# Who copies the hi part of a weight unit: ScalarE in place of GpSimd

## The reference

```
xn = rmsnorm(x) * g1;  z = xn @ w_in      # rg_x, rg_y, q, k, v, g_lr, g_out, m_a, m_b
xc = causal_conv4(rg_x)
r, i = sigmoid(blockdiag(xc)), sigmoid(blockdiag(xc))
a = exp(-8 * r * softplus(-lam));  b = sqrt(1 - a*a) * i * xc
h_t = a_t * h_(t-1) + b_t;         ya = (h * gelu(rg_y)) @ w_a
o = gated linear attention over q, k, v in chunks, 4 heads, decays from g_lr
yb = (rmsnorm(o) * gn * silu(g_out)) @ w_b
x = x + (sigmoid(m_a) * ya + sigmoid(m_b) * yb) @ w_out
u = rmsnorm(x) @ w_up;  gate, val = split(causal_conv3(u))
x = x + (gelu(gate) * val) @ w_down;      y = rmsnorm(x) * gf
```

## Time and profile before

| | |
|---|---|
| median of 3 runs | 1968.67 us (1965.29 to 1969.84) |
| the profiled execution | 1968.59 us, span 1966.8 us |
| PE busy | 1914.4 us, 97% |
| DVE busy | 906.0 us, 46% |
| POOL busy | 701.9 us, 36% |
| ACT busy | 420.9 us, 21% |
| chain that ended last | PE 92%, DVE 4%, issue 3%, ACT 1% |
| granted TensorE clock, mean | 0.988 |

### The profile page before, as it was taken

The page is one execution under the profiler, slowest core; times in us unless marked ns, Lnnn a source line. Parts: engine busy times, 40 slices in busy tenths (PEclk is TensorE's granted clock), DMA queues, the critical chain, the costliest instruction groups (busy, mean ns, idle before and its releaser), DMA issues.

```text
span 1966.8 us, 29051 instructions
## 1 busy us (share of the span) xinstructions
PE 1914.4 (97%) x11890; PEld 1885.9 (96%) x11890; DVE 906.0 (46%) x916; ACT 420.9 (21%) x480; POOL 701.9 (36%) x324
## 2 busy tenths in 40 slices
PE   7999999999999999999999999999999999999997
PEld 6999888888889999999999999999999999999997
DVE  5211277787865311141134555536253535354546
ACT  4000144555532100020011121102010101010115
POOL 3333232232234343344344333333333333334353
PEclk9999998999999999999999999999999999999999
DMA  5221123222212111131113211111111111111112
GB/s 192 87 89 43 44 88 109 89 77 91 77 43 75 43 43 53 43 130 48 48 48 125 65 44 43 44 54 44 44 44 53 43 44 45 53 43 44 53 52 86
DMA packets 48167, 127.11 MB, mean 65 GB/s; under 512 B 6952, under 2 KB 20008, under 8 KB 48080
## 3 DMA queue, kind: packets, MB, share of 16 engines
q1 hardware_dynamic: 27744, 88.39, 13.5%
q10 hardware_dynamic: 20352, 37.64, 5.5%
HBM read 108.14 MB, written 18.14 MB: 64 GB/s over the span
## 4 chain that ended last, share of the span: by engine, by line
PE 92%; DVE 4%; issue 3%; ACT 1%; DMA 0%; DVEq 0%; SPq 0%
PE acc L416 84%; PE acc L594 1%; PE acc L755 1%; PE small L514 1%; PE small L517 1%; DVE rg_xc_h L1327 1%; PE small L526 1%; DVE rg_xc_h L1324 1%; DVE rg_ext L1149 0%; PE small L607 0%; DVE gla_bc_keT L1214 0%; PE small L755 0%; PE small L489 0%; DMA x_in<-in_x 0%; PE small L533 0%
## 5 line engine op out<-in xcount | busy, mean ns | idle before, releaser
L382 POOL TENSOR_TENSOR w_hi<-w_raw,ones 128x1024 fp32r<-128x1024 f32 x149 | 288.3, 1935 | 1215.5 <-PE acc L416 1203.7
L416 PE MATMUL acc<-xn_hi,w_hi 128*128 128x346 f32 (+1 forms) x2520 | 553.8, 328 | 15.9 <-DVE xn_lo L1136 12.1
L416 PE MATMUL acc<-xn_lo,w_hi 128*128 128x346 f32 (+1 forms) x2520 | 541.8, 323 | 0.0
L416 PE MATMUL acc<-xn_hi,w_lo 128*128 128x346 f32 (+1 forms) x2520 | 540.1, 323 | 0.0
L416 PEld LDWEIGHTS acc<-xn_hi,w_hi 128*128 128x128 f32 x2520 | 427.5, 190 | 21.5 <-issue 12.9
L416 PEld LDWEIGHTS acc<-xn_lo,w_hi 128*128 128x128 f32 x2520 | 429.7, 190 | 0.0
L416 PEld LDWEIGHTS acc<-xn_hi,w_lo 128*128 128x128 f32 x2520 | 428.6, 190 | 0.0
L384 POOL TENSOR_TENSOR w_lo<-w_raw,w_hi 128x1024 fp32r<-128x1024 f32 x149 | 384.2, 2578 | 11.7
L1520 DVE TENSOR_TENSOR residual<-acc,residual 128x1032 f32<-128x1032 f32 x56 | 69.0, 1232 | 115.8 <-PE acc L416 115.8
L1491 DVE SCALAR_TENSOR_TENSOR tmp<-val_ext,ffn_params,tmp 128x1024 f32<-128x1024 f32 x48 | 97.9, 2040 | 39.4 <-ACT tmp L1069 36.6
L1491 DVE SCALAR_TENSOR_TENSOR gate_conv<-gate_ext,ffn_params,gate_conv 128x1024 f32<-128x1024 f32 x48 | 92.0, 1917 | 40.6 <-ACT gate_conv L1063 37.7
(11 more groups left out here) (216 smaller groups left out, 2082.6 us busy)
## 6 DMA issues: line engine op xcount, KB each, us to landing
w_raw<-in_w SPq DMA_DIRECT2D x153, 512.0 KB, 3.5
ha_scratch<-rg_gelu_ha ACTq DMA_DIRECT2D x8, 519.0 KB, 3.5
h<-ha_scratch ACTq DMA_DIRECT2D x8, 519.0 KB, 7.0
residual<-in_x ACTq DMA_DIRECT2D x8, 519.0 KB, 7.6
gla_qk_pair<-qk_scratch ACTq DMA_DIRECT2D x8, 512.0 KB, 5.8
smp_v_rows<-smp_v_scratch ACTq DMA_DIRECT2D x8, 512.0 KB, 6.5
out_gla_sample<-smp_state ACTq DMA_DIRECT2D x8, 512.0 KB, 3.8
smp_state<-in_gla_state ACTq DMA_DIRECT2D x7, 512.0 KB, 5.0
```

The lines of the kernel that those rows point to most:

```text
L382: nc.gpsimd.tensor_tensor(whi[s], raw[s], one, ALU.mult).then_inc(w_hi_done[s], 1)
L416: mm = nc.tensor.matmul(acc[g][:, n, 0:cw], w[s][:, t * P:(t + 1) * P], x[:, c0 + n * cw:c0 + (n + 1) * cw], start=a, stop=z)
```

## The change

The hi copies by GpSimd are kept for units 1 and 2 and for the last three. For the others ScalarE does them with an activation (Copy), in the new function w_high(u): it waits for the load of raw and for TensorE to be done with the slot's last unit, copies, and raises w_hi_done. GpSimd waits for w_hi_done and subtracts, as before. Each w_high is written at one place in ScalarE's order, so its copy is done after what stands ahead of it there: in the recurrent stage one behind line 957 and one behind line 966, in the output gates behind the Silu, in the FFN behind the bias of gate and of value. Excerpt:

```diff
@@ gpsimd
-            with pool.Fori(1, (N_UNITS - GRP) // 2) as i:
-                split(i, 0)
-                split(i, 1)
+            split(1, 0)
+
+            def low(i, s):
+                pool.wait_ge(w_hi_done[s], i + 1)
+                nc.gpsimd.tensor_tensor(wlo[s], raw[s], whi[s].bitcast(F32), ALU.subtract).then_inc(w_split[s], 1)
+            low(1, 1)
+            with pool.Fori(2, (N_UNITS - GRP) // 2) as i:
+                low(i, 0)
+                low(i, 1)
@@ scalar
+            def w_high(u, per=0, i=0):
+
+                s, n = slot_of(u), nth(u, per, i)
+                act.wait_ge(w_loaded[s], 16 * n + 16)
+                act.wait_ge(unit_done[s], n)
+                nc.scalar.activation(whi[s], raw[s], ACT.Copy).then_inc(w_hi_done[s], 1)
...
@@ scalar, recurrent stage
                 nc.scalar.activation(xc, ext[:, 3:3 + C], ACT.Identity, scale=par("w3", j), bias=par("b", j))\
                     .then_inc(xbias_ready, 1)
+                w_high(U_RG + 2, 2, j)
                 act.wait_ge(sS_ready, j + 1)
...
                 nc.scalar.activation(gy[:, late], gy[:, late], ACT.Gelu_apprx_tanh).then_inc(gelu_ready, 1)
+                w_high(U_RG + 3, 2, j)
                 plain()
@@ scalar, output gates
                     nc.scalar.activation(T[s][:, late], T[s][:, late], ACT.Silu).then_inc(silu_done, 1)
+                    w_high(U_GO + 2 + s, 2, i)
                     plain()
...
@@ scalar, ffn_block
                                      bias=fpr[:, bass.ds(3 * UB + F, 1)]).then_inc(gbias_ready, 1)
+                w_high(u + 2, per, i)
                 act.wait_ge(gconv_step, 3 * F + 3)
...
                                      bias=fpr[:, bass.ds(3 * UB + FB + F, 1)]).then_inc(vbias_ready, 1)
+                w_high(u + 3, per, i)
                 act.wait_ge(act_done, F + 1)
```

More of the change, by code:

```diff
@@ L813, in _ @@
                 for s, g in ((0, 1), (1, 0)):
+                    w_high(U_QKV + s + 2, 2, i)
                     act.wait_ge(acc_free[g], G_QKV[g] + i + 1)
@@ L889, in sample_tokens @@
                 nc.scalar.activation(t, bank[0:NS, :], ACT.Copy).then_inc(sT_ready, 1)
+            w_high(U_QKV + 10)
             ke_tokens(0, NMETA)
@@ L894, in _ @@
             load_qk(PAIR, NMETA)
+            w_high(U_QKV + 11)
+            with act.Fori(1, 4) as i:
+                w_high(U_QKV + 10, 2, i)
+                w_high(U_QKV + 11, 2, i)
             act.wait_ge(acc_free[0], G_RG[0])
@@ L1016, in _, with gate_b @@
                 gate_o(i)
-            with act.Fori(0, KB) as j:
+            def gate_b(j):
                 act.wait_ge(acc_free[1], G_B[1] + j + 1)
                 nc.scalar.activation(T[2][:, late], T[2][:, late], ACT.Tanh, scale=0.5).then_inc(tanh_done, 1)
+                w_high(U_B + 2, 2, j)
+            with act.Fori(0, KB - 1) as j:
+                gate_b(j)
+                w_high(U_B + 3, 2, j)
+            gate_b(KB - 1)
             for k in range(KB):
@@ L1027, in _ @@
                 act.dma_start(blkl(HA, k), ha_scr[k][:, late]).then_inc(hl_loaded[k], 16)
+            w_high(U_B + 3, 2, KB - 1)
             for k in range(KB):
@@ L1030, in _, with gate_a @@
                 nc.scalar.activation(blkl(HAH, k), blkl(HA, k), ACT.Copy).then_inc(hah_done, 1)
-            with act.Fori(0, KB) as j:
+            def gate_a(j):
                 act.wait_ge(acc_free[1], G_A[1] + j + 1)
                 nc.scalar.activation(T[2][:, late], T[2][:, late], ACT.Tanh, scale=0.5).then_inc(tanh_done, 1)
+                w_high(U_A + 2, 2, j)
+            with act.Fori(0, KB - 1) as j:
+                gate_a(j)
+                w_high(U_A + 3, 2, j)
+            gate_a(KB - 1)
             act.wait_ge(acc_free[1], G_OUT[1])
@@ L1038, in _ @@
                 if k == KB - 1:
-                    ready(U_OUT - 1)
+                    w_high(U_A + 3, 2, KB - 1)
                     for m in range(KB):
@@ L1045, in _ @@
             for k in range(KB):
+                w_high(U_OUT + k + 2)
                 act.wait_ge(acc_free[1 - k % 2], G_OUT[1 - k % 2] + k // 2 + 1)
@@ L1055, in _, with ffn_block @@
             norm_factor(sum2_mm, lnr2_done, r2_done, LATE)
-            def ffn_block(F, grp):
+            def ffn_block(F, grp, u, per, i):
                 plain()
@@ L1076, in _, with ffn_group, down_high @@
             GU, GD = GRP, KB // 2
-            def ffn_group(F0_, grp, half):
+            NU, ND = 2 * GRP, GRP
+            per = 2 * (NU + ND)
+            def ffn_group(F0_, grp, half, u0, i=0):
                 for f in range(GRP):
-                    ffn_block(F0_ + f, grp + f)
+                    ffn_block(F0_ + f, grp + f, u0 + 2 * f, per, i)
                     ffn_hi(half, f)
+            def down_high(u0, i, n):
+                for v in range(n):
+                    w_high(u0 + NU + v + 2, per, i)
             act.wait_ge(set_f, 4)
-            ffn_group(0, 0, 0)
+            ffn_group(0, 0, 0, U_FFN)
             gper = 2 * (GU + GD)
             with act.Fori(0, NGRP // 2 - 1) as i:
-                ffn_group(2 * GRP * i + GRP, GU + gper * i, 1)
+                ffn_group(2 * GRP * i + GRP, GU + gper * i, 1, U_FFN + NU, i)
+                down_high(U_FFN + NU, i, ND)
                 act.wait_ge(acc_free[0], G_FFN[0] + 2 * GU + GD + gper * i)
-                ffn_group(2 * GRP * i + 2 * GRP, 2 * GU + GD + gper * i, 0)
+                ffn_group(2 * GRP * i + 2 * GRP, 2 * GU + GD + gper * i, 0, U_FFN + 2 * NU + ND, i)
+                down_high(U_FFN + 2 * NU + ND, i, ND)
                 act.wait_ge(acc_free[0], G_FFN[0] + 3 * GU + 2 * GD + gper * i)
             n = NGRP // 2 - 1
-            ffn_group(GRP * (NGRP - 1), GU + gper * n, 1)
+            ffn_group(GRP * (NGRP - 1), GU + gper * n, 1, U_FFN + NU + n * per)
+            down_high(U_FFN + NU + n * per, 0, 1)
             act.preload_act_table_set(LN_EXP)
```

## The result

| | before | after |
|---|---|---|
| median of the runs beside one another | 1968.46 us (1965.29 to 1969.84) | 1940.16 us (1939.9 to 1943.3) |
| the profiled execution | 1968.59 us, span 1966.8 us | 1939.9 us, span 1938.1 us |
| PE busy | 1914.4 us, 97% | 1902.9 us, 98% |
| POOL busy | 701.9 us | 411.5 us |
| ACT busy | 420.9 us | 563.7 us |

The ratio after to before is 0.9862, interval 0.9845 to 0.9879. The forecast was 1946.0 us, so the gain is 6 us larger than it said.

What follows compares the result with a forecast made beforehand. TensorE, busy 97% of the span, was taken as the bound, with seven 3.0 us waits for the recurrent stage's masked scores. Recurrent gain, output-gate wait and FFN loss summed as 1968.6 - 29.2 + 1.35 + 5.3 = 1946.0 us; range 1934 to 1960.

Steps and rivals of the forecast that it cites:

- Removed, 3.65 us an iteration: Recurrent stage: VectorE's two ten-column steps around the scan shrink to 0.22 us each, taking 3.65 us off the chain.
- ScalarE's second copy, 0.7 us on the scores' chain: Recurrent stage: each iteration's second copy on ScalarE delays its following work by 0.7 us, all of it reaching the scores.
- Moved: the subtraction among the convolution steps, a wait of 1.0 us: Recurrent stage: the subtraction runs ahead of the second convolution step; TensorE waits about 1.0 us for the copied outputs.
- The stage: Recurrent stage: seven iterations of 39.2 us take 274.4 us instead of 303.65, a gain of 29.2 us.
- The clock: Recurrent stage: TensorE keeps full clock, granted 1.00, through the new waits of 1.0 us.
- Start of the output gates, 1.35 us once: Start of the output-gate stage: unit 35's copy stands behind the first Silu, so TensorE waits 1.35 us once.
- FFN, 7 x 0.75 = 5.3 us: FFN down groups: the subtraction gets between two VectorE steps, making the residual line 0.75 us later seven times, 5.3 us.
- Everything else at nothing: Other stages: added latency of at most 7.3 us stays under the 11.44 us a unit lasts, so no cost.
- subtraction behind the steps: Rival, chance 0.13: VectorE keeps second and third convolution steps together; new waits and most of unit 35's vanish; 1932 us.
- Half clock stays: Rival, chance 0.11: the recurrent stage's new waits still bring the clock down, 2.3 us each of seven times; 1962 us.
- the gain is eaten: Rival, chance 0.05: the recurrent stage's wait for copied outputs replaces the whole one removed; time within 0.2% of before.
- slower: Rival, chance 0.07: the recurrent stage's small steps don't wait for GpSimd, so nothing comes off the chain; 1983 us.

Runs made afterwards that it cites:

- e5: Changed kernel with ScalarE's first copy of each recurrent iteration moved ahead of the wait for the block's result; 1949.73 us, ratio 0.9901.
- e6: Kernel before with GpSimd's slot 1 splits held behind the convolution in the recurrent stage, and a like hold in each FFN group; 1934.89 us, ratio 0.9824.
- e4: Changed kernel with GpSimd's subtraction held until the convolution steps are done, in the recurrent stage (slot 1) and the FFN; 1935.17 us, ratio 0.983.
- e1: Kernel before with hi copies moved to ScalarE only for the units split in the recurrent stage; 1936.38 us, ratio 0.9836.
- e3: Kernel before, all splits on GpSimd, which in the recurrent stage begins slot 1's split only after the iteration's convolution steps; 1932.41 us, ratio 0.9822.
- e8: Kernel before with GpSimd setting the hi buffer to a constant instead of copying, for slot 1 in the recurrent stage; 1942.54 us, ratio 0.9869.
- e7: Changed kernel with the second unit of each recurrent iteration split by GpSimd alone again; 1939.92 us, ratio 0.9855.

## Why the prediction was right, and where its sizes were off

The mechanism, the stage, the place of each new wait and the clock came as forecast; the measured gain was 6 us larger, since the new waits are about half of what was summed. Two of its signs came out small by that: the wait for the outputs at 0.44 us instead of about 1, and those for the residual at 0.6 and less instead of 0.7 to 0.8. By its steps:

- *Removed, 3.65 us an iteration.* Right: (1.79 - 0.16) + (2.30 - 0.14) = 3.79. ScalarE's copy takes 1.05 us as reckoned, by the mean of 147.
- *ScalarE's second copy, 0.7 us on the scores' chain.* Right in kind, too dear. Line 990 starts 1.92 us after the start of line 986, where the same two stood 1.38 apart before: 0.54 us late, not 0.7. The scores are ready 0.45 us ahead of TensorE and were 3.01 behind it, so they gained 3.46 of the 3.79; only 0.33 us of the delay reached them. The forecast let all of it through because it saw hardly a pause on ScalarE. One is there: in the kernel before line 977 starts at 442.51, 1.31 us after line 973, behind the second gate product on TensorE, which ends there at 442.37; in the kernel after line 998 starts 1.17 us after line 994. That wait takes up 0.14 us of the delay.
- *Moved: the subtraction among the convolution steps, a wait of 1.0 us.* The place is right to the step: it asks during the first and holds up the second. The size is 0.44 us. The steps begin 1.28 us after the first score product instead of 1.7, because the scores are early by what the last point says; and they take 415.10 - 409.03 = 6.07 us instead of 6.4, since the subtraction holds VectorE from 410.33 to 412.56, 2.23 us, where the sum had the whole 2.40 and a full 1.30 for the step behind it. Against that stand 0.15 us between the end of the output copy and the state updates, which the sum left out.
- *The stage.* 269.34 us instead of 274.4. The gain is 303.65 - 269.34 = 34.3 us, not 29.2: this is 5.1 of the 6 us.
- *The clock.* Right. The granted 1.00 holds from 240 to 556 us. It had been argued from a single idle of 1.85 us; the seven waits of 1.5 in e5 now show it for waits of that length. For longer ones e6 shows that no such argument from a single idle holds: 2.54 us kept the clock and 2.24 us didn't.
- *Start of the output gates, 1.35 us once.* Right: 1.25 before the first matmul with the new unit. It begins with the Silu on ScalarE at 558.63, 1.07 us long. VectorE, ScalarE, GpSimd and TensorE there, a timeline each:

```profile
559.74 1.30 DVE L1450 SCALAR_TENSOR_TENSOR tmp<-v_o,params,tmp 128x1038 f32<-128x1038 f32 x1 [2.50 <-ACT tmp L1029]
```

```profile
559.61 1.04 ACT L784 ACTIVATE w_hi<-w_raw 128x1024 fp32r<-128x1024 f32 x1
```

```profile
560.73 2.55 POOL L393 TENSOR_TENSOR w_lo<-w_raw,w_hi 128x1024 fp32r<-128x1024 f32 x1 [21.13 <-ACT w_hi L784]
```

```profile
563.41 0.74 PE L422 MATMUL acc<-xn_hi,w_hi 128*128 128x346 f32 x3 [1.25 <-POOL w_lo L393]
```

- *FFN, 7 x 0.75 = 5.3 us.* Seven waits in the right place, but smaller: 3.9 us in the view of the weight loads against 0.5 before, so 3.4 us (the matmuls' own view has 1.7 us in six; in the recurrent stage it is the weight loads' view that agrees with the time lost). VectorE and GpSimd in one down group, beside the earlier trace rows and the last of the earlier trace rows:

```profile
1232.83 4.63 DVE L1535 SCALAR_TENSOR_TENSOR tmp<-val_ext,ffn_params,tmp 128x1024 f32<-128x1024 f32 x2 [1.57 <-ACT tmp L1103]
```

```profile
1233.71 2.66 POOL L393 TENSOR_TENSOR w_lo<-w_raw,w_hi 128x1024 fp32r<-128x1024 f32 x1 [8.63 <-ACT w_hi L784]
```

The pair of steps takes 4.63 us where it took 4.19, 0.44 more, and the sum had 4.94: the same 0.3 too much for a held step as in the recurrent stage.

- *Everything else at nothing.* Right: of the waits for a split only the one of 1.3 us was added.
- *Not in the forecast:* the clock's stretch at the entry of the stage, 6.8 us in this profile and 3.4 in that of before, costs 1.7 us here. Together, 34.3 - 1.3 - 3.4 - 1.7 = 27.9 us of the 28.7 by which the spans differ. Of the other 0.8 us, 0.6 is in the waits for xn_lo at the start of the kernel, 11.5 us here and 12.1 before; over the eleven profiles they vary from 11.2 to 12.1.

Of the rivals, "subtraction behind the steps" was the nearest after the forecast: e4 makes it real and has 1935.17 us, where the rival's sum said 1932. Its profiled execution has 1936.81: the stretch of 13.7 us at the entry instead of 3.4 is worth up to 5 us there, and the wait of 1.3 at unit 35, which the rival let go for the most part, stayed. "Half clock stays" fell with the granted 1.00 of the kernel after, and e5 keeps the clock with waits of 1.5; "the gain is eaten" fell with waits of 0.44 us for the outputs in place of 3; "slower" fell with e1 and e3.

## What to carry to other kernels

When a tiny VectorE operation lasts some us, look at what GpSimd reads at that moment: an operation with two inputs in SBUF and a reading GpSimd instruction take turns, and whichever asks while the other runs goes next. The cure is to move GpSimd's instruction in time, to where VectorE copies out of PSUM or is idle; one wait in GpSimd's own order (e3) gave 35 us, while giving the work to another engine gave 28. That brought three new waits, of 3.0 us in the recurrent stage, 1.3 at unit 35 and 3.4 in the FFN, and the last two come with the 131 copies that hadn't been in anybody's way. Cost such a move stage by stage, since here 16 of 147 copies held all of the gain and the rest a loss of 4 to 6 us.

## What the runs showed of the hardware that had not been expected

- A wait of 3.0 us on TensorE among small matmuls brought the clock down to its lower level (1.2 GHz) each of seven times, for 3.4 us (four times) or 6.8 us (three times), and cost some 2.0 us on average on top of itself. Waits of 1.4 to 1.6 us, fourteen times in e5 and e8, left it at 2.4 GHz. In between the length alone doesn't decide: in e6 an idle of 2.24 us was followed by 3.4 us at the lower level, and one of 2.54 us by none.
- What the waits of the recurrent stage cost is in the view of the weight loads, not in that of the matmuls: over the seven iterations of the recurrent stage e5, e8, after and e7 take 12.3, 11.3, 3.0 and 2.1 us more than e3, where the weight loads' entries are 12.6, 11.5, 3.1 and 2.1 and the matmuls' 10.5, 9.5, 1.4 and none.
- The clock at the entry of the recurrent stage, behind a stretch in which TensorE was busy for 2.40 of 4 us in the kernel after, is at its lower level for 3.4, 6.8 or 13.7 us, and for one and the same kernel for 6.8 or 13.7.
- A held VectorE step costs less than the GpSimd instruction that holds it: the second and third convolution steps take 4.61 us with the subtraction beside them and 2.75 without (e4), 1.86 more, for a subtraction that takes 2.41 alone. It asks before the first step ends, and it runs through the 0.15 us by which VectorE pauses between the first two steps anyway. The Trainium skill calls the shared port pair "an exclusive lock" ("SBUF — State Buffer", section "Who interferes with whom"). The rows agree in kind; the sum that takes the whole duration as lost comes out too high.
